# First blocks of a layer's first group selected from token rows in SBUF, a seventh weight chunk, and a re-ordered routing chain

## The reference

```python
for i in range(DEPTH):                      # 2 layers
    mix = rg_lru_block(...) if i == 0 else pool_mixer(...)
    x = layer_norm(DEEPNORM_ALPHA * x + mix, ln_g[i, 0], ln_b[i, 0])
    ffn = hier_moe(x, ...)
    x = layer_norm(DEEPNORM_ALPHA * x + ffn, ln_g[i, 1], ln_b[i, 1])

def hier_moe(x, wg, bg, we, be, w_gate_up, w_down):
    lg = xt @ wg + bg                        # 4 groups
    gsel, p_sel = argmax(lg), max(softmax(lg))
    le_sel = (xt @ we + be).reshape(t, 4, 4)[arange(t), gsel]
    topv, topi = lax.top_k(le_sel, 2)        # 2 of the group's 4 experts
    wt = softmax(topv) * p_sel
    hu = einsum('td,edf->tef', xt, w_gate_up)     # 16 experts, 2048 x 1024
    hg, hv = split(hu, 2)
    act = silu(hg) * hv * gates[..., None]
    return einsum('tef,efd->td', act, w_down)     # 16 experts, 512 x 2048
```

## Time and profile before

| what | value |
|---|---|
| median of 3 runs | 1477.49 us (1477.11 to 1479.07) |
| the profiled execution | 1478.47 us |
| its span in the trace | 1476.7 us |
| PE busy | 1397.5 us (95%) |
| DVE busy | 523.4 us (35%) |
| ACT busy | 365.0 us (25%) |
| POOL busy | 27.8 us (2%) |
| DMA | 489.05 MB, mean 331 GB/s |

### The profile page before, as it was taken

The page is one execution under the profiler, slowest core; times in us unless marked ns, Lnnn a source line. Parts: engine busy times, 40 slices in busy tenths (PEclk is TensorE's granted clock), DMA queues, the critical chain, the costliest instruction groups (busy, mean ns, idle before and its releaser), DMA issues.

```text
span 1476.7 us, 20987 instructions
## 1 busy us (share of the span) xinstructions
PE 1397.5 (95%) x9148; PEld 780.9 (53%) x9148; DVE 523.4 (35%) x1084; ACT 365.0 (25%) x562; POOL 27.8 (2%) x36
## 2 busy tenths in 40 slices
PE   8999999999899999999898999889999999999895
PEld 8999999999643333243233338654343333234331
DVE  5777888643332021022002117625024013102302
ACT  5567666432310120021012002311021012001101
POOL 0000001000000000000000000000000000000000
PEclk9999999999889999999999999989999999999997
DMA  9846453843589999999999987669999999999992
GB/s 303 272 143 193 138 183 97 276 163 151 179 326 381 427 405 429 426 425 427 427 427 414 427 338 292 226 216 385 426 416 414 428 427 423 427 428 428 415 429 92
DMA packets 94567, 489.05 MB, mean 331 GB/s; under 512 B 8408, under 2 KB 64664, under 8 KB 67320
## 3 DMA queue, kind: packets, MB, share of 16 engines
q1 hardware_dynamic: 85072, 466.22, 79.0%
q10 hardware_dynamic: 6730, 12.66, 3.0%
q0 software_dynamic: 2672, 8.82, 1.6%
HBM read 481.95 MB, written 16.04 MB: 337 GB/s over the span
## 4 chain that ended last, share of the span: by engine, by line
PE 73%; DMA 16%; DVE 7%; issue 2%; ACT 1%; ACTq 0%; DVEq 0%; POOL 0%; SPq 0%; POOLq 0%
PE ps L1198 21%; PE ps L1219 20%; DMA ring<-in_moe_w_down 14%; PE ps L1128 5%; PE ps L993 4%; PE ps L994 4%; PE ps L995 4%; PE ps L1080 2%; PE ps L1081 2%; PE ps L1082 2%; PE ps L1152 2%; PE ps L1282 1%; DMA ring<-in_lru_w_in 1%; PE ps L1115 1%; DMA xtok<-x_rows,src_now 1%
## 5 line engine op out<-in xcount | busy, mean ns | idle before, releaser
L1198 PE MATMUL ps<-ring,xsel 128*64 128x512 f32 x2048 | 469.6, 609 | 16.9 <-DMA ring<-in_moe_w_gate_up 16.0
L1219 PE MATMUL ps<-ring,work 128*32 128x512 f32 x3072 | 346.2, 595 | 9.9 <-DMA ring<-in_moe_w_down 9.9
L1198 PEld LDWEIGHTS ps<-ring,xsel 128*64 128x64 f32 x2048 | 141.9, 139 | 307.9 <-issue 274.2
L1219 PEld LDWEIGHTS ps<-ring,work 128*32 128x32 f32 x3072 | 91.7, 109 | 221.4 <-issue 201.6
L1795 DVE SCALAR_TENSOR_TENSOR arena<-arena,ps 64x512 f32<-64x512 f32 x32 | 21.7, 678 | 501.6 <-ACT work L851 501.6
L993 PE MATMUL ps<-operands,whi 128*128 128x288 f32 x512 | 153.6, 300 | 4.0 <-DVE ring_lo L1355 3.4
L994 PE MATMUL ps<-ring_lo,whi 128*128 128x288 f32 x512 | 153.2, 299 | 0.0
L995 PE MATMUL ps<-operands,ring_lo 128*128 128x288 f32 x512 | 152.1, 297 | 0.0
L1355 DVE TENSOR_TENSOR ring_lo<-ring,whi 128x1024 fp32r<-128x1024 f32 x96 | 115.7, 1221 | 63.6 <-ACT whi L646 63.4
L646 ACT ACTIVATE whi<-ring 128x1024 fp32r<-128x1024 f32 x96 | 100.3, 1057 | 129.2 <-PE ps L995 71.5
L850 ACT ACTIVATE arena<-ps 64x512 f32<-64x512 f32 x32 | 18.9, 589 | 403.5 <-PE ps L1198 403.4
(11 more groups left out here) (347 smaller groups left out, 1199.7 us busy)
## 6 DMA issues: line engine op xcount, KB each, us to landing
ring<-in_moe_w_gate_up SPq DMA_DIRECT2D x128, 2048.0 KB, 18.0
ring<-in_moe_w_down SPq DMA_DIRECT2D x64, 2048.0 KB, 18.7
ring<-in_lru_w_in SPq DMA_DIRECT2D x15, 2048.0 KB, 10.0
ring<-in_lru_w_out SPq DMA_DIRECT2D x8, 2048.0 KB, 8.9
x_rows<-xtok ACTq DMA_DIRECT2D x4, 1024.0 KB, 3.9
ring<-in_pool_w SPq DMA_DIRECT2D x4, 1024.0 KB, 14.3
xtok<-in_x_prompt SPq DMA_DIRECT2D x2, 1024.0 KB, 7.9
ring<-in_lru_w_in SPq DMA_DIRECT2D x4, 512.0 KB, 12.9
```

The lines of the kernel that those rows point to most:

```text
L1198: last = mm(ps[half * ES:(half + 1) * ES, e % 2, :], xsel[:, k, e * ES:(e + 1) * ES], wt[:, half * 512:(half + 1) * 512], start=(k == 0), ...
L1219: last = mm(ps[rows:rows + QB, 2 + r, :], act[:, e % 2, f * W + slots0:f * W + slots0 + QB], wt[:, d * 512:(d + 1) * 512], start=start, st ...
```

## The change

Six things.

1. `select_first`: pairs 0 and 1 of a layer's first window are selected not from the gathered rows but from the token rows in SBUF, in three matmuls per block (one for each tile of tokens) with a selection matrix `first_sel` (3 tiles x 256 columns). `select_rows` does pairs 2 to 7 as before.
2. A seventh chunk: chunk 6 of a layer's first window goes to `spare`, the first two rows of `xtok` (free once the gather has landed and pairs 0 and 1 are selected). Chunks 7 to 12 then wait for one chunk less. `XS` moves to `xtok`'s third row, the tail's token rows to `xsel`'s back half. `ZS`, inside `spare`, is written after part 28; in layer 1 `ln_b`'s row also waits for that on ScalarE's queue. Ring numbers after it shift by one.
3. Routing: `first_max` works on 15 sets of 4 at once (the group's logits and all four groups' experts), and the chain behind the count is cut to what `one_hot` needs. `link.also` counts an instruction without waiting for it.
4. Between `one_hot(0, 1)` and `src_now` VectorE makes `first_rank`, `first_sel` and then all of `settle()`, which holds what was cut out of the chain.
5. `stay_awake(8)` with 288 columns behind the slots gives way to `stay_awake(2)` with 256 columns ahead of them; gates go to part 5, over to part 7.
6. In head 0 of the mixer `decay_rates` (VectorE) and its Exp (ScalarE) come after the loop over parts instead of inside it.

```diff
-C_POOL = C_MOE0 + NG * PER_WIN
+C_POOL = C_MOE0 + NG * PER_WIN - 1
...
-FIRST_GATES_AT = 1
-OVER_AT = 3
+FIRST_GATES_AT = 5
+OVER_AT = 7
+DIRECT = 2
...
+def ring_no(base, p, first):
+
+    return base + p if first and p < NSLOT else base + p - 1
...
+    def also(self, ins):
+        self.n += 1
+        ins.then_inc(self.sem, 1)
...
-        XS, ZS = xtok[0:W, 0, :], xtok[0:W, 1, :]
+        XS, ZS = xtok[0:W, 2, :], xtok[0:W, 1, :]
+        tail_rows = xsel_f[0:TS, KD // 2 * NE * ES:KD // 2 * NE * ES + D]
+        token_rows = [xtok[:, 0, :], xtok[:, 1, :], tail_rows]
+        first_sel = carve(work, 0, 3, NE * ES)
...
+                        if first and p == NSLOT:
+                            eng.wait_ge(rows_in[l], 16)
+                            eng.wait_ge(rows_turned[l], DIRECT)
+                            eng.dma_start(spare, src).then_inc(spare_in, 16)
+                            p += 1
+                            continue
...
+                            if first and NSLOT < p <= 2 * NSLOT:
+                                held = p - NSLOT - 1
+                            else:
+                                held = p - NSLOT + (NG if first and l == 1 and p < NSLOT else 0)
...
                     if p == 9:
                         eng.wait_ge(uc_ready, h + 1)
                         eng.activation(UC_hi[:, :, :], UC_all[:, :, :], ACT.Copy).then_inc(uc_hi_ready, 1)
-                        if h == 0:
-                            eng.wait_ge(derived, 1)
-                            eng.activation(sp[1][:, :], sp[0][:, :], ACT.Exp, scale=-1.0).then_inc(lam_exp, 1)
+                if h == 0:
+                    eng.wait_ge(derived, 1)
+                    eng.activation(sp[1][:, :], sp[0][:, :], ACT.Exp, scale=-1.0).then_inc(lam_exp, 1)
...
-                for dst, name in zip(res_row[l][l:], ("ln_g", "ln_b")[l:]):
-                    eng.dma_start(dst, A[name][l, 0:1, :].to_broadcast([W, D])).then_inc(ln_row_in, 16)
+                if l == 0:
+                    for dst, name in zip(res_row[0], ("ln_g", "ln_b")):
+                        eng.dma_start(dst, A[name][0, 0:1, :].to_broadcast([W, D])).then_inc(ln_row_in, 16)
...
+                            eng.wait_ge(parts_used, seq * PARTS_WIN + (parts0 + (NSLOT + 1) * PARTS_CHUNK))
+                            eng.dma_start(res_row[1][1], A["ln_b"][1, 0:1, :].to_broadcast([W, D])).then_inc(ln_row_in, 16)
...
+                def select_first(q):
+
+                    for b in range(2):
+                        k = 2 * q + b
+                        for i, (t0, m) in enumerate(TILES):
+                            last = mm(ps[:, 6 + q % 2, b * 256:(b + 1) * 256], feature_block(token_rows[i], k)[0:m, :],
+                                      first_sel[0:m, i, :], start=(i == 0), stop=(i == 2))
+                    last.then_inc(rows_turned[l], 1)
...
+                eng.wait_ge(tr_act[1 + l], 7)
+                stay_awake(2)
                 eng.wait_ge(P_ready, 2 * l + 1)
                 eng.wait_ge(tr_act[1 + l], 12)
                 slots(0, range(1), 2 + NE, 0)
                 eng.wait_ge(tr_act[1 + l], 12)
                 if l == 0:
                     eng.wait_ge(cstT_ready, 1)
-                stay_awake(8)
+                eng.wait_ge(first_sel_ready, l + 1)
...
-                        if h == 0:
-                            decay_rates()
+                if h == 0:
+                    decay_rates()
...
+            def first_max(out, v, m):
+
+                link(V.tensor_reduce(m, v, AX.X, ALU.max))
+                link(TT_(out, v, m.unsqueeze(2).to_broadcast([128, 15, 4]), ALU.is_equal))
+                link(TT_(out, out, firstw[:, :].unsqueeze(1).to_broadcast([128, 15, 4]), ALU.mult))
+                link(V.tensor_reduce(first_at, out, AX.X, ALU.max))
+                link(TT_(out, out, first_at.unsqueeze(2).to_broadcast([128, 15, 4]), ALU.is_equal))
...
+                first_max(best, groups, top)
+                TT_(r4[0][:, :, :], lg, tops[:, :, 0:1].to_broadcast([128, 3, 4]), ALU.subtract).then_inc(ex_in, 1)
+                link.also(TT_(Gh, best.rearrange(of_tile, i=3)[:, :, 0, :], bc(valid[:, :, :], 4), ALU.mult))
+                link(STT(masked, best, -1e30, groups, ALU.mult, ALU.add))
+                first_max(second, masked, runner)
+                link(TT_(masked, best, second, ALU.add))
...
+                    link.also(STT(lprod[:, i, :], ahead[:, i, NG:], 1.0, members[:, i, NG:], ALU.add, ALU.mult))
                 link(TT_(gw[:, :, :], Gh, ahead[:, :, 0:NG], ALU.mult))
+                link.also(V.tensor_reduce(pos[:, :, 0], gw[:, :, :], AX.X, ALU.add))
+                link(V.tensor_reduce(rank_vals, lprod[:, :, :].rearrange("p i (g j) -> p i j g", g=4), AX.X, ALU.add))
+                link.also(TT_(at_slot[:, :, :], slotno[:, :, :], pos[:, :, :], ALU.add))
                 link(V.tensor_reduce(most[:, :, 0], rank_vals, AX.X, ALU.max))
+                link(STT(both_fit[:, :, :], most[:, :, :], float(ES), valid[:, :, :], ALU.is_le, ALU.mult))
+                link(STT(fit[:, :, :], pos[:, :, :], float(W), both_fit[:, :, :], ALU.is_lt, ALU.mult))
...
+                def settle():
+
+                    link.also(STT(slotno[:, :, :], at_slot[:, :, :], 1.0, fit[:, :, :], ALU.add, ALU.mult))
+                    link(TT_(over[:, :, :], valid[:, :, :], fit[:, :, :], ALU.subtract))
+                    link.also(TS_(slotno[:, :, :], slotno[:, :, :], -1.0, None, ALU.add))
+                    TT_(over_g[:, :, :], Gh, bc(over[:, :, :], 4), ALU.mult).then_inc(oh_ready, 1)
+                    for i in range(3):
+                        link.also(TT_(pair[:, i, :].rearrange("p (g j) -> p g j", g=4), best[:, 5 * i + 1:5 * i + 5, :],
+                                      Gh[:, i, :].unsqueeze(2).to_broadcast([128, 4, 4]), ALU.mult))
+                    link(V.tensor_reduce(les[:, :, :], members[:, :, NG:].rearrange("p i (g j) -> p i j g", g=4), AX.X, ALU.add))
+                    link(V.tensor_reduce(E1[:, :, :], pair.rearrange("p i (g j) -> p i j g", g=4), AX.X, ALU.add))
+                    link(TT_(gate4[:, :, :], les[:, :, :], E1[:, :, :], ALU.subtract))
...
                 one_hot(0, 1)
-                link(TT_(over_g[:, :, :], Gh, bc(over[:, :, :], 4), ALU.mult))
-                signal(oh_ready, 1)
+                link(TT_(r4[3][:, :, :], rank_vals, bc(fit[:, :, :], 4), ALU.mult))
+                link(TT_(first_rank[:, :, :], r4[3][:, :, :], Gh[:, :, 0:1].to_broadcast([128, 3, 4]), ALU.mult))
+                for i in range(3):
+                    ins = TT_(first_sel[:, i, :].rearrange("p (e j) -> p e j", e=NE),
+                              iota_f[:, 1:ES + 1].unsqueeze(1).to_broadcast([128, NE, ES]),
+                              first_rank[:, i, :].unsqueeze(2).to_broadcast([128, NE, ES]), ALU.is_equal)
+                ins.then_inc(first_sel_ready, 1)
+                settle()
                 eng.wait_ge(slots_full, 3 * l + 1)
```

More of the change, by code:

```diff
@@ L263, in encoder_step @@
         Gh = members[:, :, 0:NG]
+        best, second, masked = [carve(arena, 2816 + i * 60, 15, 4) for i in range(3)]
+        top, runner, first_at = [carve(arena, 2996 + i * 15, 15) for i in range(3)]
+        pair = carve(arena, 3044, 3, 16)
         th = carve(arena, 0, FE)
         P = carve(arena, FE, 3, WINS * W)
-        XS, ZS = xtok[0:W, 0, :], xtok[0:W, 1, :]
+        XS, ZS = xtok[0:W, 2, :], xtok[0:W, 1, :]
+        tail_rows = xsel_f[0:TS, KD // 2 * NE * ES:KD // 2 * NE * ES + D]
+        token_rows = [xtok[:, 0, :], xtok[:, 1, :], tail_rows]
+        first_sel = carve(work, 0, 3, NE * ES)
+        first_rank = carve(arena, 3092, 3, NE)
         prow = carve(sqm, 0, 3, 128)
@@ L286, in encoder_step @@
         yT = carve(xtf, 0, KD, T)
+        spare = xtf[:, 0:2 * D]
         PX = PW + TP + PW + TS
@@ L1156, in window @@
                     for i, (kind, e, q) in enumerate(WINDOW_PARTS):
-                        n = base + i // PARTS_CHUNK
+                        p = i // PARTS_CHUNK
+                        n, in_spare = ring_no(base, p, first), first and p == NSLOT
+                        held = spare if in_spare else ring_at(n)
                         if first and i == FIRST_GATES_AT:
@@ L1181, in window @@
                                     eng.wait_ge(act_ready[l], w * (NE + 1) + (r - 1))
-                                select_rows(w, r)
+                                if first and r < DIRECT:
+                                    select_first(r)
+                                else:
+                                    select_rows(w, r, DIRECT if first else 0)
                         if ahead and i in NEXT_AT:
@@ L1590, in moe @@
+                pos, most, over, fit, both_fit, at_slot = r1[0], r1[1], r1[4], r1[8], r1[7], r1[6]
+                link.also(TT_(runner, runner, top, ALU.subtract))
                 link(TT_(gw[:, :, :], Gh, gidx[:, :].unsqueeze(1).to_broadcast([128, 3, 4]), ALU.mult))
```

(14 more changed lines are left out.)

100 lines of the change are left out of this document (40 added, 60 removed).

## The result

The change made the kernel slower: 1488.03 us (median of 6 runs, 1483.8 to 1490.65) against 1476.5 (6 runs, 1471.61 to 1479.07) for the kernel before, timed beside it. The ratio is 1.0079, 95% interval 1.0062 to 1.0096. The forecast was 1478.1 with a range up to 1482.0. The profiled execution took 1486.47 us for a span of 1484.7, 8.0 us more than the span of 1476.7 before; the traces explain those 8.0 us, not the whole 11.5 between the medians.

A forecast was written before the change was run, and what follows sets the result against it. A layer's first window was taken as bound by TensorE, later ones by the DMA queue. Terms 1.2 - 0.05 - 0.6 = +0.6 us on the median 1477.49 gave 1478.1 us, range 1473.5 to 1482.

The forecast's parts named there:

- the clock of the direct selection: First windows: twelve selection matmuls take 7.4 us, or up to 12, beside the gather; part 0 moves -0.05 and -0.6 us.
- After part 0 the same parts, selections, gates and over work follow in another order: 0: Rest of each layer's first window behind part 0: the reordered work costs or gains nothing, 0 us.
- The decay rates: Mixer head 0: gelu 1.66 us late, so TensorE restarts later; cost 0.83 to 1.66 us, taken as 1.2.
- seven DMA issues on ScalarE: Between heads 0 and 1: part of the tight chain behind the late gelu, which restarts TensorE 1.66 us later.
- The seventh chunk at 0: First windows: an extra chunk's lead gains 0, as no DMA wait is on the path before 584; bound 9.8 us.
- The shorter routing and the later src_now: Routing before the gather: src_now 0.4 us later in layer 0, 0.14 us earlier in layer 1.
- ScalarE still waits for rows_in: Before block 0 in first windows: ScalarE waits for the gather and its DMA issues, so part 0 isn't freed; chance 0.59.
- Slower: head 0's late restart keeps the clock low: Rival, head 1's start: TensorE idle 5.1 us, low stretch as long again costs 3.5 us more; 1482.1 us, chance 0.13.
- The low clock stretches in the first windows shrink: Rival, behind the over matmuls: layer 0's low stretch goes, saving 3.3 us; 1474.8 us, chance 0.2.
- Its sign that would show the forecast wrong: Different count of low-clock stretches between 390 and 450 or 970 and 1020, moving the result 1.5 to 3.3 us each.

The follow-up runs named there:

- Experiment 4: The kernel before without its eight wide stay_awake matmuls, nothing of the change: 1486.07 us, ratio 1.0065.
- experiment 5: The kernel after with eight wide matmuls put back ahead of the direct selection: 1481.08 us, ratio 1.0035.
- experiment 6: The kernel after with four more wide matmuls ahead of the slots and two behind them, in idle time: 1477.01 us, ratio 1.0002.
- experiment 11: Experiment 7 with the decay rates after head 0's loop again, as in the change: 1473.72 us, ratio 0.9972.
- experiment 7: Experiment 6 with ScalarE's first evacuation ahead of its wait for the gather and decay rates back in head 0's window: 1470.86 us, ratio 0.9963.
- experiment 3: The kernel after without the direct selection, eight wide matmuls back ahead of the gathered one: 1478.7 us, ratio 1.0014.
- experiment 8: Experiment 3 with the decay rates back in head 0's window: 1477.08 us, ratio 1.0003.
- experiment 1: The kernel after with decay rates and their Exp back inside head 0's loop over parts: 1484.25 us, ratio 1.0048.
- experiment 2: The kernel after with the seventh chunk held back until the first chunk has been used: 1485.16 us, ratio 1.0073.
- experiment 10: Experiment 7 with the seventh chunk held back until the first chunk has been used: 1470.44 us, ratio 0.9948.

## Why the prediction was wrong

**The step that failed** is the clock of the direct selection. The prediction put it as "In layer 0 they run from 388.75 at first at the low level and end at about 397.7; in layer 1 from 962.1 [...] to at most 971.2, if the first four run at the low level. Both fit beside the gather." It had the bound in hand ("or up to 12") and took the low price for the first four matmuls only. In layer 0 all twelve ran at the low level and ended at 402.25: 12.74 us, and part 0 3.77 us later (0.78 of it already there at A). In layer 1 all but the first 0.9 us was low, 12.17 us in all up to 978.33. Part 0 was 5.70 us later there, 4.24 of it already there near the end of that layer's mixer (948.49 against 944.25 for the same sums), so 1.5 of its own; the rest of the loss from B to C lies in the parts behind it that still ran at the low level, up to 987.5. The term "After part 0 the same parts, selections, gates and over work follow in another order: 0" failed with it. Behind that stood a second omission. The eight wide matmuls of the kernel before were given no price of their own, since they lay under the gather. They were what brought the clock up before the first parts. Experiment 4 shows what they were worth, 0.65% or 9.6 us of 1477; experiments 5 and 6 show that with such work ahead of it the direct selection runs at the high level. Both halves belong to the cause: the work that brought the clock up was gone, and the twelve matmuls, put first, did not bring it up. Six matmuls in the idle time give back 11 us.

**The decay rates** were right in mechanism and mis-sized. VectorE idles 1.56 us for high part 11, and the gelu operation starts at 51.47 instead of 51.21 in an execution that was 1.4 us ahead up to there: 1.66 us late, as worked out. But the term was 1.2 us (0.83 to 1.66), and the gap at head 1's start grew by 4.0 us, from 3.43 to 7.46. The missing 2.4 us are the third n_rows issue, 3.85 us instead of 1.47. The prediction counted "seven DMA issues on ScalarE" at their old durations, though the step moved them past an issue of SyncE. Part of it came back: in the kernel after the low stretch there ends at 72.78, 3.9 us after TensorE's restart at 68.86, before at 71.94, 5.7 us after it. The Trainium skill's "TensorE: Matmul & The Clock Gate", section "What's actually happening", had been read as saying that a later restart pushes the rise back; here the rise moved by 0.84 us when the restart moved by 2.64. The net price by the ratios is 1.3 to 1.6 us (experiments 11 and 7, 3 and 8); the pair after and 1 says 4.6. All three point the same way, but in none of them are the intervals apart, so that the decay rates cost time is seen in the traces and their net price is not well known.

**The seventh chunk at 0** was right, for the reason given: no wait for DMA before 584, and experiments 2 and 10 show no loss without it.

**The shorter routing and the later src_now** came out as worked out. Relative to the count, src_now is 0.3 us later in layer 0 (forecast 0.4). It gains nothing that can be measured: experiment 8 is at 1.0003.

**"ScalarE still waits for rows_in"** was right as a statement and was not what ended last. The gather held ScalarE until 397.90 and TensorE until 402.25. Once the clock was mended it did end last, for 1.49 and 1.78 us, and taking it away was worth 4.4 us (11 against 6).

**The rivals.** "Slower: head 0's late restart keeps the clock low" ended on the right side for the wrong place: TensorE was idle there for 7.46 us, longer than the rival's 5.1, and the low stretch at head 1 still did not grow (6.83 us in both kernels). "The low clock stretches in the first windows shrink" looked at the right thing and had the sign wrong. It argued that "eight stay_awake matmuls give way to twelve real ones", as if the twelve would do the eight's work for the clock. They did not. Its sign that would show the forecast wrong, another count of low stretches, was the one that spoke: between 380 and 450 the kernel after had two, not three, but 27.3 us long in sum instead of 17.1.

## What to carry to other kernels

Work that only fills an idle engine has a price and a worth in the clock of what follows. Before it is removed or shortened, read the granted clock of the stretch behind it, and let the range of the forecast hold the case that the first real work after idle time runs at the low level from end to end, not only for its first few instructions. Where the filling ends matters too: six matmuls more gave 11 us in one kernel, and six more cost 5 in the other, where the filling was over 3.66 us before the real work.

A DMA issue that moves in time is to be compared with the issues of the other queues around its new place, not only with its own engine's neighbours.

## What the runs showed of the hardware

- **A high clock is kept by work that does not raise a low one.** With filling work just ahead the twelve matmuls of the direct selection ran at 1.00 throughout (8.0 us, experiments 6 and 7). In layer 1 of the kernel after, behind 1.79 and 0.59 us of idle time, they began at the high level and it fell 0.9 us later. From the low level TensorE worked from 389.51 on without a pause, and the clock stayed at 0.50 until 407.2. Eight wide matmuls with fixed weights, started at the low level at 389.17, had it up before 394.4. The Trainium skill's "TensorE: Matmul & The Clock Gate", section "What's actually happening", has activity release the clock; the 17.7 us of unbroken activity up to 407.2 here did not. What sets the two kinds apart (weights loaded anew for each matmul, 32-row tiles among them) was not tried one by one and stays open.
- **A matmul on 32 rows costs no less than one on 128 rows.** In the kernel after, from the start of one group of rows to the next, the two matmuls on 128 rows (four records) took 2.03 us (399.06 to 401.09), the one on 32 rows (two records) 1.16 us (401.09 to 402.25). The third token tile holds a ninth of the rows and takes over a third of the time.
- **A DMA issue can hold its engine more than twice as long** (3.85 instead of 1.47 us) where another queue's 2 MB load was issued 0.9 us ahead of it. The order of the two issues went with the duration in all thirteen traces that had both, and so did the place of the decay rates, so the two are not told apart. That the load itself is the cause was not tried by moving the load alone; the second of the three issues, also behind the load, took 0.69 us in either kind.
